# Start addresses of the normed rows', the up products' and the down product's operands, shifted against the weights

## The reference

```python
def reference(x, mem, ...):
    x = first_block(x, mem, ...)     # hybrid layer
    return second_block(x, ...)      # second layer with an FFN, and a final norm

# first layer
h = rms_norm(x, norm_g)
proj = h @ w_in                      # 2048 x 16512
ya = chunked_band_attention(aq, ak, av, a_rel_bias) * silu(az)
yb = rwkv7_time_mix(...) * silu(bz)
yc = memory_cross_attention(cq, mk, mv) * silu(cz)     # mk, mv from mem @ w_mem_kv
merged = sigmoid(ga) * (ya @ w_up_a) + sigmoid(gb) * (yb @ w_up_b) + sigmoid(gc) * (yc @ w_up_c)
x = x + merged @ w_o

# second layer
h = rms_norm_2(x, norm1_w);  proj = h @ w_in_2
mixed = g0 * (attention @ w_br_attn) + g1 * (gla @ w_br_gla) + g2 * (conv @ w_br_conv)
x = x + mixed @ w_out
h2 = rms_norm_2(x, norm2_w)
x = x + (silu(h2 @ w_ffn_gate) * (h2 @ w_ffn_up)) @ w_ffn_down      # width 5632
return rms_norm_2(x, final_norm_w)
```

## Time and profile before

| what | value |
|---|---|
| median of 3 runs | 2960.38 us (2960.34 to 2961.88) |
| the profiled execution | 2960.85 us |
| its span | 2959.1 us |
| mean granted clock of TensorE | 0.995 |
| PE busy | 2907.4 us (98%), 18226 matmuls |
| DVE, ACT, POOL busy | 1609.6, 1336.8 and 67.2 us |
| read from HBM | 513.39 MB, 174 GB/s over the span |

### The profile page before, as it was taken

How to read it: one execution, slowest core, us unless ns; L and a number is a source line. 1 busy time by engine, 2 the same in 40 slices (tenths; PEclk the granted TensorE clock), 3 DMA queues, 4 the chain that set the end, 5 groups by cost and what they waited for, 6 DMA issues and landing times.

```text
span 2959.1 us, 42670 instructions
## 1 busy us (share of the span) xinstructions
PE 2907.4 (98%) x18226; PEld 2514.0 (85%) x18226; DVE 1609.6 (54%) x1851; ACT 1336.8 (45%) x1527; POOL 67.2 (2%) x173
## 2 busy tenths in 40 slices
PE   7999999999999999999999999999999999999998
PEld 7978898888988888898998889888888888888886
DVE  4555656556656556554554466554655545545444
ACT  4443543444554454444444444444444444444443
POOL 4000000001000000000000000000000000000000
PEclk9999999999999999999999999999999999999999
DMA  6343434566665655656556555666666666666664
GB/s 200 115 143 112 132 116 136 152 190 184 224 195 182 190 163 186 194 159 189 165 163 200 165 139 161 198 197 194 197 188 186 190 192 186 190 193 201 194 195 151
DMA packets 356178, 518.30 MB, mean 175 GB/s; under 512 B 18288, under 2 KB 137220, under 8 KB 355220
## 3 DMA queue, kind: packets, MB, share of 16 engines
q1 hardware_dynamic: 355220, 512.37, 58.0%
q0 software_dynamic: 768, 3.20, 0.4%
HBM read 513.39 MB, written 2.11 MB: 174 GB/s over the span
## 4 chain that ended last, share of the span: by engine, by line
PE 94%; DVE 2%; ACT 1%; issue 1%; POOL 1%; DMA 0%; SPq 0%; DVEq 0%; POOLq 0%; ACTq 0%
PE gp L1617 23%; PE gp L1619 23%; PE gp L1618 23%; PE gp L1626 6%; PE gp L1627 6%; PE gp L1628 6%; PE ps L1792 4%; PE ps L1674 1%; PE ps L1749 1%; PE ps L1780 1%; DVE w_lo L1023 1%; POOL arena L527 0%; DVE arena L1017 0%; ACT w_hi L631 0%; PE ps L1734 0%
## 5 line engine op out<-in xcount | busy, mean ns | idle before, releaser
L1023 DVE TENSOR_TENSOR w_lo<-w_raw,w_hi 128x1024 fp32r<-128x1024 f32 (+2 forms) x976 | 1169.1, 1204 | 1001.9 <-ACT w_hi L631 998.1
L631 ACT ACTIVATE w_hi<-w_raw 128x1024 fp32r<-128x1024 f32 (+2 forms) x976 | 1010.2, 1040 | 1127.8 <-PE gp L1619 897.8
L1617 PE MATMUL gp<-w_hi,h_hi 128*128 128x512 f32 x2112 | 833.0, 394 | 1.7 <-DVE w_lo L1023 1.3
L1619 PE MATMUL gp<-w_lo,h_hi 128*128 128x512 f32 x2112 | 822.6, 390 | 0.0
L1618 PE MATMUL gp<-w_hi,h_lo 128*128 128x512 f32 x2112 | 822.3, 389 | 0.0
L1626 PE MATMUL gp<-h_hi,w_hi 128*128 128x256 f32 x1696 | 496.2, 293 | 9.5 <-DVE w_lo L1023 6.6
L1627 PE MATMUL gp<-h_lo,w_hi 128*128 128x256 f32 x1696 | 481.2, 284 | 0.0
L1628 PE MATMUL gp<-h_hi,w_lo 128*128 128x256 f32 x1696 | 481.1, 284 | 0.0
L1617 PEld LDWEIGHTS gp<-w_hi,h_hi 128*128 128x128 f32 x2112 | 396.6, 188 | 84.3 <-DVE w_lo L1023 1.7
L1619 PEld LDWEIGHTS gp<-w_lo,h_hi 128*128 128x128 f32 x2112 | 396.5, 188 | 83.4
L1618 PEld LDWEIGHTS gp<-w_hi,h_lo 128*128 128x128 f32 x2112 | 396.7, 188 | 80.5 <-issue 0.5
(11 more groups left out here) (283 smaller groups left out, 1779.4 us busy)
## 6 DMA issues: line engine op xcount, KB each, us to landing
w_raw<-in_w_in SPq DMA_DIRECT2D x384, 512.0 KB, 4.2
w_raw<-in_w_ffn_gate SPq DMA_DIRECT2D x88, 512.0 KB, 4.5
w_raw<-in_w_ffn_up SPq DMA_DIRECT2D x88, 512.0 KB, 4.4
w_raw<-in_w_ffn_down SPq DMA_DIRECT2D x88, 512.0 KB, 4.1
w_raw<-in_w_in SPq DMA_DIRECT2D x136, 256.0 KB, 3.2
w_raw<-in_w_in SPq DMA_DIRECT2D x128, 192.0 KB, 2.9
w_raw<-in_w_mem_kv SPq DMA_DIRECT2D x32, 512.0 KB, 4.3
w_raw<-in_w_o SPq DMA_DIRECT2D x32, 512.0 KB, 4.3
```

Of the source, the lines that this page charges most:

```text
L631: act.activation(w_hi[:, slot, 0:size], w_raw[:, slot, 0:size], ACT.Copy).then_inc(sem("hi_done"), 1)
L1023: dve.tensor_tensor(w_lo[:, slot, 0:size], w_raw[:, slot, 0:size], w_hi[:, slot, 0:size].bitcast(F32), ALU.subtract)\
L1617: pe.matmul(o, xh, wh, start=(k == 0), stop=False)
L1619: ins = pe.matmul(o, xh, wl, start=False, stop=(k == last_k))
```

## The change

Three gaps are put into the layout. `sb_past` lays down a filler buffer at a multiple of 512 bytes, as long as `PAST` says for the name's first letter, and the buffer right behind it: `h_hi` begins 256 bytes past a multiple of 512, `y_hi` 96, `f_hi` 224. The lo buffers, whose align argument is dropped, follow directly and have the same remainder, as the sizes are multiples of 512. `mem_lo`, `mem_first` and `arena` lie behind y without an alignment of their own, and so at 96 past. The ring's buffers stay at the multiples. To make room the arena loses 128 values; `l_up` moves from block 81 of it to block 18, which the second attention's `q_v` uses before, and so its load is issued behind that attention.

```diff
         ROW = 4 * P
+        PAST = {'h': 256, 'y': 96, 'f': 224}
+
+        def sb_past(name, shape, dt, where=ctx):
+            at = PAST[name[:name.index("_")]]
+            if at:
+                sb(f"gap_{name}", [P, at // 4], F32, where, ROW)
+            return sb(name, shape, dt, where, 32 if at else ROW)
...
-        h_hi = sb("h_hi", [P, KD, T], F32R, align=ROW)
-        h_lo = sb("h_lo", [P, KD, T], F32R, align=ROW)
+        h_hi = sb_past("h_hi", [P, KD, T], F32R)
+        h_lo = sb("h_lo", [P, KD, T], F32R)
...
-        y_hi = sb("y_hi", [P, KB, T], F32R, y_ctx, ROW)
-        y_lo = sb("y_lo", [P, KB, T], F32R, y_ctx, ROW)
-        ARENA = 83 * 256
+        y_hi = sb_past("y_hi", [P, KB, T], F32R, y_ctx)
+        y_lo = sb("y_lo", [P, KB, T], F32R, y_ctx)
+        ARENA = 165 * 128
         with ExitStack() as mem_ctx:
-            mem_lo = sb("mem_lo", [P, KD, T], F32R, mem_ctx, ROW)
-            mem_first = sb("mem_first", [P, KD // 2, T], F32R, mem_ctx, ROW)
-        arena = sb("arena", [P, ARENA], F32, y_ctx, ROW)
+            mem_lo = sb("mem_lo", [P, KD, T], F32R, mem_ctx)
+            mem_first = sb("mem_first", [P, KD // 2, T], F32R, mem_ctx)
+        arena = sb("arena", [P, ARENA], F32, y_ctx)
         y_ctx.close()
-        f_hi = sb("f_hi", [P, KF, T], F32R, align=ROW)
-        f_lo = sb("f_lo", [P, KF, T], F32R, align=ROW)
+        f_hi = sb_past("f_hi", [P, KF, T], F32R)
+        f_lo = sb("f_lo", [P, KF, T], F32R)
...
-        l_down, l_up, l_v = area(80, T), area(81, 512), area(56, 2, BW)
+        l_down, l_up, l_v = area(80, T), area(18, 512), area(56, 2, BW)
...
             pool.wait_ge(sem("cross_lo"), 12)
-            pool.dma_start(l_up[0:16, :], dram["gla_w_up_2"]...).then_inc(sem("up_landed"), 16)
...
             pool.wait_ge(sem("y_lo"), KB + 20)
+            pool.dma_start(l_up[0:16, :], dram["gla_w_up_2"]...).then_inc(sem("up_landed"), 16)
             pool.memset(l_at[:, :, :], 0.0)
```

More of the change, by code:

```diff
@@ L595, in _ @@
             pool.wait_ge(sem("cross_lo"), 12)
-            pool.dma_start(l_up[0:16, :], dram["gla_w_up_2"].rearrange("l r n -> (l r) n")).then_inc(sem("up_landed"), 16)
             for tt in range(2):
@@ L611, in _ @@
             pool.wait_ge(sem("y_lo"), KB + 20)
+            pool.dma_start(l_up[0:16, :], dram["gla_w_up_2"].rearrange("l r n -> (l r) n")).then_inc(sem("up_landed"), 16)
             pool.memset(l_at[:, :, :], 0.0)
```

## The result

The changed kernel takes 2979.93 us (2979.41 to 2981.58), the one before 2960.38: a ratio of 1.0066, 95% interval 1.0049 to 1.0083. It is slower by 19.6 us, where 48 us less was forecast. The profiled execution's span goes from 2959.1 to 2978.2 us, 19.1 more, and that is what the trace can explain. The mean granted clock is 0.995 in both.

The account below looks back on a forecast made before the run. PE's start-to-start matmul intervals were taken as the bound. From 2960.85 us, 48 less for the new distances and 0 for the other parts gave 2912.4, so 2912 us, with a range of 2807 to 2975.

Parts of the forecast that it names:

- What bounds the kernel: PE, busy 98% of the span; time can only come out of the start-to-start intervals of its matmuls.
- Is the surcharge a matter of addresses: Split products pay 11.0 ns that plain ones don't; supposedly set by the distance between loaded and moving addresses.
- the rival "nothing changes": All split products: the 13.3 ns beside the columns is a fixed cost, time stays 2960 us; chance 0.20.
- The hypothesis: Load and moving stream hinder each other where their addresses coincide in some period, and their distance decides how much.
- part 1: The shifted h, y, mem and f products, 14016 in all: the new distances save 48 us.
- the four prices of the distance: Bounds for 14016 products: 154 us less, 0, 74 us more, or 48 us less; the last was taken.
- the price of 2 and 6 ns less from the shortest durations: 8928 row products at 2 ns and 5088 column products at 6 ns: 18 and 30.5 us less.
- The ten intervals of the earlier trace: Disturbed pace after plain products, 232 ns against 226.7; if steady, 5.3 ns each, 74 us more.
- The rival that ended slower: Streams meet in mid-load in row products of h and f: 5.3 ns each, 3000 to 3035 us; chance 0.20.
- The Trainium skill's formula: Matmul interval N / 2.4 + 2.5 ns at full clock; if split products reached it, 152 us.
- Its rule of two independent read ports: Loading the next weights on PE takes no bandwidth from the running matmul; by it the time stays 2960 us.
- Parts 2 to 4: Moved ident, blk, eye and arena; later load of gla_w_up_2; another engine taking over: each 0 us.

Follow-up runs that it names:

- e2: Changed kernel with only y shifted (96 bytes, with mem_lo, mem_first and the arena), h and f at 0; 2974.07 us, 1.0044 of the kernel before.
- e3: Changed kernel with only f shifted (224 bytes), h and y at 0; 2968.06 us, 1.0027 of the kernel before.
- e4: Changed kernel with weights, h, y and f all starting 96 bytes past a multiple of 512; 2959.65 us, 0.9999 of the kernel before.
- e6: Changed kernel with PAST alone set to h 64, y 160, f 16 bytes (lo part of f 32); 3006.41 us, one execution.
- e10: Changed kernel with y at 96, h and f at 0, loading 64 of 128 operand columns in row products except first and last k tiles; 2987.29 us.
- the scan: Six kernels, each the changed kernel with other distances in PAST for h, y and f, one profiled execution each; 2999.05 to 3015.94 us.
- e1: Changed kernel with only h shifted (256 bytes), y, mem, arena and f at multiples of 512; 2959.41 us, 0.9997 of the kernel before.
- e5: Changed kernel with PAST alone set to h 128, y 32, f 64 bytes; 3007.35 us, one execution.
- e15: Changed kernel with weights placed by block kind: column products 48 bytes apart, row products at distance 0 with both sides at 48; 2999.67 us, 1.0130.

## Why the prediction was wrong, point by point

- **What bounds the kernel**: right. PE's intervals are the time, and a nanosecond in them arrives in full: 19.0 us of intervals for 19.1 us of span.
- **Is the surcharge a matter of addresses**: right that the distance matters (e2, e3, e4), which the rival "nothing changes" denied. Its place was partly wrong: for h, which carries 11424 of the 14016 products, the shift of 256 is worth 0. The hypothesis left the period open; the sum treated all three shifts as equal. The pace of e6's columns, 113.3 or 117.8 ns at one distance, and e10, where a shorter load costs more at distance 0, show that more than the distance is in it.
- **The step that failed** is the choice in part 1 among the four prices of the distance, "TensorE's pairs at the multiples of 512 start together, which a hypothesis of coinciding reads makes one of the worse distances, so a gain is likelier than a loss", and with it the price of 2 and 6 ns less from the shortest durations, 48 us less in all. Measured were 0.1 ns or less at h, 7.4 ns more at y and mem and 6.6 ns more at f, 19 us more in all. For 512 moving columns, starting together is, with 256, the best of the fifteen settings tried, and 233 ns is the common pace. The shortest durations of the earlier trace rows were rare records, 387 ns in 22 of 2112 and 277 ns in 4 of 1696, and no steady pace of the trace before. At no distance was such a pace (224.7) seen in rows; in columns three long stretches at 64 bytes reached it (113.3, where 114 was expected), a distance that the change doesn't have. The ten intervals of the earlier trace rows, 232 ns on average, came nearer: they were listed as the dear end of the range and lie within 2 ns of the common pace of the scan. They run from 224 to 236 ns, though, and are no steady pace either, so the nearness may be chance.
- **The rival that ended slower** had the direction and nearly the price (5.3 ns, measured 7.4 and 6.6), but its place was h and f, and its mechanism, an overtaking in mid-load, isn't shown: h at 256 would be overtaken half-way through its load as well, and pays nothing.
- **The Trainium skill's formula** ("TensorE: Matmul & The Clock Gate", Back-to-back issue gap, where it is called the isolated single-MM gap), 215.8 and 109.2 ns, was reached at no distance; the lowest steady paces here are 226.7 in rows and 113.3 in columns. That plain products come near it, as the prediction says, holds of the fixed part alone, 2.3 ns beside 2.5: with 256 columns they take 215.6 ns. Its rule of two independent read ports (same page, Step-by-step: what each phase is for) would have the distance do nothing; y at 96 costs 13.4 us where the weights lie at 0 (e2) and nothing where they lie at 96 too (e4), so the measurement decides against drawing that from it.
- **Parts 2 to 4** at 0: right. e1 has ident, blk and the moved load where the change has them and takes 0.9997 of the time before; with the arena at 96 too, 160 of the transposes of the arena are listed at 299 ns on average, before at 298, and the next groups at 272 as before. ACT and DVE kept their durations, and PE's waits for w_lo stayed at a few us.

What stays open is the mechanism: why a long moving stream has its shortest pace at distances of 0 and 256, why a short one gains at 32 and 64 bytes, and what picks between two paces at one distance. The traces list starts and modelled ends, not the reads; that two reads hinder each other is a hypothesis that the runs neither show nor exclude.

## What to carry to other kernels

Read the pace of back-to-back matmuls as start to start, by operand and by stretch, and compare it with the columns streamed; a busy share of 98% hid 13 ns in each of 14000. If a buffer has to move, keep the distance of the loaded and the moving side at a multiple of 256 bytes and both at multiples of 32 where 512 columns of split products move; where 256 move, try 32 bytes apart. These are the places that this kernel's runs found best, and no rule beyond them. A scan is cheap when operands have stages of their own: one execution with a profile gives three distances at once.

## What the runs showed of the hardware that was not expected

- A matmul of a split product with 512 moving columns has its shortest pace, 226.7 ns, at distances 0 and 256, and 229 to 234 elsewhere. The longer paces are steady too: 233 and 234 ns in turn at 64 (f in e5), a repeating pattern of seven intervals between 231 and 238 at 96. The pace of 226.7 is lost as well when half as many columns are loaded (229.9).
- The same instruction with 256 moving columns has its slower pace at 0 (119.8 to 120.0) and its lowest mean at 32 (117.0).
- Two stretches of the same instruction at the same distance can differ, each steady: 113.3 and 117.8 ns at 64 bytes in columns (e6), 230.0 and 233.3 ns in rows with both sides at 48 (e15).
- Equal starts are not enough: both sides at 48 or 24 bytes cost 3 to 7 ns in a row product, both at 32 or 96 nothing.
